# Two-block transformer on one core: residual pieces split before they are scaled, and weight refills issued earlier

## What is computed

```python
x = half_ffn(x, ffn_norm[l, 0], ...)
h = rmsnorm(x, mix_norm[l])
x = x + (mixer_gla_rglru(h, ...) if l == 0 else mixer_hgrn2(h, ...))
x = half_ffn(x, ffn_norm[l, 1], ...)
gate = sigmoid(rmsnorm(x, ple_norm[l]) @ ple_gate[l])
x = x + gate * (p[l] @ ple_proj[l])        # "PLE" below
```

## Time and profile before

| | us |
|---|---|
| runs | 2873.18, 2870.72, 2865.55 (median 2870.72) |
| the profiled execution | 2868.27 |
| its span | 2866.5 |
| TensorE matmul busy | 2717.7 (95%) |
| TensorE weight load busy | 2623.7 |
| DVE busy | 1380.7 (48%) |
| ACT busy | 1493.7 (52%) |
| GpSimd busy | 2206.3 (77%) |
| granted TensorE clock, mean | 0.975 |

### The profile page before, as it was taken

How to read it: one execution, slowest core, us unless ns; L and a number is a source line. 1 busy time by engine, 2 the same in 40 slices (tenths; PEclk the granted TensorE clock), 3 DMA queues, 4 the chain that set the end, 5 groups by cost and what they waited for, 6 DMA issues and landing times.

```text
span 2866.5 us, 60073 instructions
## 1 busy us (share of the span) xinstructions
PE 2717.7 (95%) x21805; PEld 2623.7 (92%) x21812; DVE 1380.7 (48%) x2501; ACT 1493.7 (52%) x2269; POOL 2206.3 (77%) x1681
## 2 busy tenths in 40 slices
PE   8999999999999999999989989999999899898997
PEld 8999988889999989898889989998999899788997
DVE  2125435646556554525556554346433733735335
ACT  4444455555555545455465554457545644555445
POOL 8876766757988967666858968978898699667994
PEclk9999999999999999999999999999999999999998
DMA  6544434434554544433434544544555355444552
GB/s 242 183 169 151 142 124 135 153 118 155 184 175 158 187 143 170 133 133 133 162 118 155 183 147 162 183 147 159 170 184 187 126 189 185 135 135 148 188 183 78
DMA packets 123000, 452.12 MB, mean 158 GB/s; under 512 B 13650, under 2 KB 13650, under 8 KB 122196
## 3 DMA queue, kind: packets, MB, share of 16 engines
q1 hardware_dynamic: 121104, 441.43, 45.8%
q10 hardware_dynamic: 1732, 8.39, 0.8%
HBM read 448.72 MB, written 1.05 MB: 157 GB/s over the span
## 4 chain that ended last, share of the span: by engine, by line
POOL 45%; PE 25%; issue 23%; DVE 5%; ACT 2%; POOLq 0%; DVEq 0%; ACTq 0%
POOL wl L372 23%; POOL wl L373 22%; PE R L407 6%; PE R L411 6%; PE R L410 6%; PE Y L407 1%; PE Y L411 1%; PE Y L410 1%; DVE M L2260 1%; DVE XLB L1904 0%; ACT wh L1140 0%; PE Y L647 0%; PE R L512 0%; DVE G L2259 0%; PE R L570 0%
## 5 line engine op out<-in xcount | busy, mean ns | idle before, releaser
L372 POOL TENSOR_TENSOR wl<-raw,wh 128x512 fp32r<-128x512 f32 x836 | 1112.3, 1331 | 639.1 <-ACT wh L1140 632.9
L407 PE MATMUL R<-XHB,wh 128*128 128x256 f32 (+1 forms) x4264 | 1218.8, 286 | 15.9 <-DVE XLB L2279 6.2
L411 PE MATMUL R<-XHB,wl 128*128 128x256 f32 (+1 forms) x4264 | 1209.5, 284 | 0.0
L410 PE MATMUL R<-XLB,wh 128*128 128x256 f32 (+1 forms) x4264 | 1205.6, 283 | 0.0
L373 POOL TENSOR_TENSOR wl<-raw,wh 128x512 fp32r<-128x512 f32 x836 | 1144.4, 1369 | 0.0
L1140 ACT ACTIVATE wh<-raw 128x1024 fp32r<-128x1024 f32 x836 | 877.3, 1058 | 298.8 <-PE R L407 218.8
L407 PEld LDWEIGHTS R<-XHB,wh 128*128 128x128 f32 x4264 | 810.9, 190 | 23.7 <-POOL wl L373 10.4
L410 PEld LDWEIGHTS R<-XLB,wh 128*128 128x128 f32 x4264 | 814.1, 191 | 1.8 <-issue 1.0
L411 PEld LDWEIGHTS R<-XHB,wl 128*128 128x128 f32 x4264 | 812.5, 191 | 0.0
L407 PE MATMUL Y<-BH,wh 128*128 128x256 f32 x1408 | 398.0, 283 | 1.3 <-DVE BL L1828 1.3
L411 PE MATMUL Y<-BH,wl 128*128 128x256 f32 x1408 | 396.4, 282 | 0.0
(11 more groups left out here) (402 smaller groups left out, 3187.9 us busy)
## 6 DMA issues: line engine op xcount, KB each, us to landing
raw<-in_stream SPq DMA_DIRECT2D x836, 512.0 KB, 3.3
G<-in_wcmp ACTq DMA_DIRECT2D x2, 2048.0 KB, 7.8
G<-in_mem ACTq DMA_DIRECT2D x2, 1024.0 KB, 7.2
TB<-in_table SPq DMA_DIRECT2D x1, 1312.0 KB, 12.4
X<-in_x SPq DMA_DIRECT2D x2, 512.0 KB, 5.1
out_dram<-X ACTq DMA_DIRECT2D x4, 256.0 KB, 2.2
WS<-in_mix_w ACTq DMA_DIRECT2D x2, 256.0 KB
G<-in_p ACTq DMA_DIRECT2D x2, 256.0 KB, 3.3
```

Of the source, the lines that this page charges most:

```text
L372: pool.tensor_tensor(wl[:, s, 0:512], raw[:, r, 0:512], wh[:, s, 0:512].bitcast(F32), ALU.subtract)
L407: i = pe.matmul(o, wh[w], hi, start=start, stop=False, skip_group_check=True)
L410: pe.matmul(o, wh[w], lo, start=False, stop=False, skip_group_check=True)
L411: i = pe.matmul(o, wl[w], hi, start=False, stop=stop, skip_group_check=True)
```

## The change

The pieces go unscaled to the first six blocks at ln1, gla and hgrn: three together, then the sum of squares, then three plain blocks, the last of which tells ACT of each piece that it has read (`piece_read`). DVE scales these six outputs by the root, and scales X into X or W8 by a copy of the root in PSUM (RS); ACT and DVE then overwrite XH and XL with the scaled pieces, from which the rest is made. In `gla` the order of chunks becomes lr, k, xr, xg. PLE's norm goes too: the projection comes first, the gates are made of unscaled pieces in BH and BL, and each gate output is scaled, passed through tanh and used in its PSUM bank; in layer 0 the next feed-forward's pieces are made per chunk (and its first product takes lead=6). `add_y` makes pieces as it adds; the last ln4 interleaves its pieces. `split_early` issues one refill ahead of a seam's pieces, on the end of the stage before.

```diff
-    return dict(xr=0, lr=4, k=5, xg=7, q=11, g=13)
+    return dict(lr=0, k=1, xr=3, xg=7, q=11, g=13)
...
+            def unscaled_six(hi, lo, width):
+
+                together(3, hi, lo, split_ready, width)
+                need(sq_added, 3)
+                for c in range(2):
+                    i = pe.matmul(SQ, ONES, W8[:, c, :], start=c == 0, stop=c == 1, skip_group_check=True)
+                i.then_inc(sum_ready, 1)
+                for _ in range(2):
+                    dense(hi, lo, width=width)
+                dense(hi, lo, width=width, passed=piece_read)
...
+                unscaled_six(XHB, XLB, T + 2)
                 together(3, XH, XL, split_ready)
-                for c in range(3, Z_N):
+                for c in range(3, 9):
+                    aside(c)
+                for c in range(9, Z_N):
                     dense(XH, XL)
                     aside(c)
...
+                unscaled_six(XH, XL, T)
                 together(3, XH, XL, split_ready)
-                for _ in range(3):
-                    dense(XH, XL)
                 evicted(c["lr"])
...
-                for _ in range(5):
+                for _ in range(2):
                     dense(XH, XL)
                 need(lconv_split)
...
-                together(3, XH, XL, split_ready)
-                for _ in range(5):
-                    dense(XH, XL)
+                unscaled_six(XH, XL, T)
+                together(2, XH, XL, split_ready)
                 tokens_major(XH, XL)
...
+            def split_early(s, value):
+
+                n = t.n["hi"]
+                act.wait_ge(raw_landed[n % RAW], t.up(("raw", n % RAW), 16))
+                act.wait_ge(s, value)
+                t.up("begun")
+                t.up("hi")
+                act.activation(wh[:, n % SPLIT, :], raw[:, n % RAW, :], ACT.Copy).then_inc(hi_done, 1)
...
+            def piece_again(c, src):
+
+                act.wait_ge(piece_read, t.up(piece_read))
+                give_dve(act.activation(XH[:, c, :], src, ACT.Copy))
...
+                late_root(0, keep=True)
+                skip(6)
+                split_next()
+                split_next()
+                biased(0)
+                biased(1)
+                step(biased(2))
+                split_next()
+                for c in range(4):
+                    i = shifted(c)
+                step(i)
+                aside(2)
+                for c in range(4, DC):
+                    i = shifted(c)
+                step(i)
+                split_next()
+                biased(3)
+                split_next()
+                biased(4)
+                for c in range(DC - 1):
+                    piece_again(c, X[:, c, :])
+                biased(5)
+                last_again(X[:, DC - 1, :])
...
+                late_root(1)
+                skip(6)
+                for _ in range(5):
                     split_next()
-                    skip(1)
-                column(c["lr"])
-                column(c["k"])
+                for j in range(DC - 1):
+                    need(x_scaled)
+                    piece_again(j, W8[:, j, :])
+                need(x_scaled)
+                last_again(W8[:, DC - 1, :])
                 split_next()
+                skip(1)
                 o = ready_of("gla", "gate")
...
+                late_root(1)
                 need(lb_shifted)
                 act.activation(LB[:, 0:2, :], LB[:, 0:2, :], ACT.Exp).then_inc(lb_exp, 1)
-                for c in range(8):
+                split_next()
+                split_next()
+                for c in range(3):
+                    from_dve()
+                    forget(c)
+                split_next()
+                split_next()
+                from_dve()
+                forget(3)
+                split_next()
+                from_dve()
+                forget(4)
+                for c in range(DC - 1):
+                    need(x_scaled)
+                    piece_again(c, W8[:, c, :])
...
-                norm(DC, xs, False, 1.0 / D, 1, None, XH, made=projected)
...
+                late_root(1)
                 for c in range(DC):
                     split_next()
+                    need(gate_scaled)
                     m, o = chunk()
-                    take(act.activation(W8[:, c, :], o[:, 0:T], ACT.Tanh, scale=0.5), m)
...
+                    give_dve(act.activation(o[:, 0:T], o[:, 0:T], ACT.Tanh, scale=0.5))
+                    if l + 1 < DEPTH:
...
+                        piece(c, following)
...
+            def scaled_again(gain):
+
+                step(dve.tensor_copy(RS, S3[:, 0:T]))
+                for c in range(DC):
+                    give(stt(W8[:, c, :], X[:, c, :], col(gain, c), RS, ALU.mult, ALU.mult), x_scaled)
+
+            def low_again(c, src):
+
+                from_act()
+                give_pe(tt_(XL[:, c, :], src, XH[:, c, :].bitcast(F32), ALU.subtract))
...
+                for c in range(3):
+                    scaled(c)
+                scaled_again("mix_g1")
+                scaled(3)
+                scaled(4)
+                for c in range(DC - 1):
+                    low_again(c, W8[:, c, :])
+                scaled(5)
+                low_again(DC - 1, W8[:, DC - 1, :])
                 need(lb_exp)
...
                 for c in range(DC):
-                    skip(1)
+                    m, o = chunk()
+                    give(tt_(o[:, 0:T], o[:, 0:T], S3[:, 0:T], ALU.mult), gate_scaled)
                     from_act()
-                    step(stt(M[:, c, :], W8[:, c, :], 1.0, M[:, c, :], ALU.add, ALU.mult))
-                    give_act(stt(X[:, c, :], M[:, c, :], 0.5, X[:, c, :], ALU.mult, ALU.add))
+                    step(stt(o[:, 0:T], o[:, 0:T], 1.0, M[:, c, :], ALU.add, ALU.mult))
+                    take(stt(X[:, c, :], o[:, 0:T], 0.5, X[:, c, :], ALU.mult, ALU.add), m)
```

More of the change, by code:

```diff
@@ L1208, in pieces @@
                     piece(c, gain)
+                    if c == 3 and early is not None:
+                        early()
             def last_splits(gain):
@@ L1253, in ffn @@
                     skip(1)
-                split_next()
+                if not early:
+                    split_next()
                 if kind != "first":
@@ L2001, in sharpen, with norm @@
                 take(stt(y, u, 1.5, y, ALU.add, ALU.mult), m)
-            def norm(n, src, mean, scale, eps, gain, bias, hi, lo, between=0, behind=0):
+            def norm(n, src, mean, scale, eps, gain, bias, hi, lo, between=0, behind=0, made=None):
                 if mean:
@@ L2038, in norm @@
                     low(n - 1)
+                elif made is not None:
+                    made(n - 1)
             def softmax(u, a):
@@ L2121, in rope, with scaled @@
                     return tt_(Z[:, c, :], Z[:, c, :], S1[:, :], ALU.add)
+                def scaled(c):
+                    m, o = chunk()
+                    step(tt_(Z[:, c, :], o[:, 0:T], S3[:, 0:T], ALU.mult))
+                    take(tt_(BQ[:, c:c + 1], o[:, T:T + 1], col(f"b_in{l}", c), ALU.add), m)
+                    dve.sem_inc(dve_act, 1)
+                    t.up(dve_act)
+                for c in range(3):
+                    scaled(c)
+                step(dve.tensor_copy(RS, S3[:, 0:T]))
+                for c in range(DC):
+                    give(stt(X[:, c, :], X[:, c, :], col(f"ln1_g{l}", c), RS, ALU.mult, ALU.mult), x_scaled)
+                for c in range(3, 5):
+                    scaled(c)
+                for c in range(DC - 1):
+                    low_again(c, X[:, c, :])
+                scaled(5)
+                low_again(DC - 1, X[:, DC - 1, :])
                 step(ts_(NB_IN[:, :], col(f"b_in{l}", Z_N, Z_GATES), 0.5, None, ALU.mult))
@@ L2342, in gla @@
                         take(i, m) if d == 3 else step(i)
+                late_root(RMS_EPS)
+                for z in (c["lr"], c["k"], c["k"] + 1):
+                    m, o = chunk()
+                    take(tt_(Z[:, z, :], o[:, 0:T], S3[:, 0:T], ALU.mult), m)
+                scaled_again("mix_g0")
+                conv(0)
+                conv(1)
+                for j in range(4):
+                    low_again(j, W8[:, j, :])
+                conv(2)
+                for j in range(4, DC):
+                    low_again(j, W8[:, j, :])
+                conv(3)
                 dve.sem_inc(lconv_done, 1)
```

183 lines of the change are left out of this document (118 added, 65 removed).

## The result

The changed kernel takes 2889.57 us (median; 2886.85 to 2890.68), the kernel before 2869.05 beside it: ratio 1.0070, 95% interval 1.0058 to 1.0082. It is slower by some 20 us where the forecast said 2868, no change; 2889.6 lies above the range, past its end of 2884. The profiled execution has a span of 2888.9 us against 2866.5 before.

The account below looks back on a forecast made before the run. PE was taken to set the pace, GpSimd's blocks ready just ahead, with PE's idle time at the seams. Terms -1.0 + 5.0 + 6.5 - 3.0 - 4.5 - 3.0 gave 0.0 against 2868.3 us; range 2846 to 2884.

Parts of the forecast that it names:

- forecast case: All seams: gains and losses of the terms cancel, 2868 us; chance 0.50, own range 2857 to 2880.
- rival 2: Mixer entries: second three-block product starves, block 9 after t = 19.5; 2880 us, 2888 with hgrn's chain slow; chance 0.17.
- ln1, -0.5 each: ln1, both layers: earlier start nearly lost waiting for block 9, at t = 16.6 from the sum of squares' start; -1.0 together.
- gla, +5.0: gla entry: five refills in a row, then the gate and block 11's late refill delay the token-major blocks; +5.0 us.
- hgrn, +6.5: hgrn entry: DVE's bounding of f starts later, behind scalings and low parts, delaying ACT's exps; +6.5 us.
- ln4, -3.0: ln4 of layer 1 into the feed-forward: early refill no longer falls between low parts; -3.0 us.
- PLE of layer 0, -4.5: PLE, layer 0: projection starts at once without the norm, gate chunks then 3.3 us each; -4.5 us.
- PLE of layer 1, -3.0: PLE, layer 1: the same without new pieces, last gate chunk earlier, tail of 16.4 us kept; -3.0 us.
- Early refills ahead of ln3 and ln4, 0: Three entries, ln3 and ln4 of layer 0: fourth block was ready in time, centring waits for sums; 0.
- Rival 1: Entries: refills keep up and the entries' gains stay; with half of the waits gone -22, 2846 us; chance 0.28.
- Rival 3: Unscaled entries: PE waits at the same instants, chunks waiting for the root hold the banks; within 3 us of 2868; chance 0.05.
- The estimate with an added drain at each table load (2874): Four roots that hold up refills: a 1.38 us drain per table switch, 5.5 us more, 2874 us; rejected from the trace.

Follow-up runs that it names:

- Late_early: Changed kernel with the early refill of gla and hgrn moved from behind the fourth unscaled piece to behind the last one; 2883.94 us, ratio 1.0055.
- f_delayed: Kernel before the change, with eight extra two-SBUF-operand subtractions on DVE in hgrn ahead of the bounding of f; 2872.07 us, ratio 1.0013.
- all_back: Changed kernel with the gla, hgrn and both ln1 entries as before; PLE, last ln4 and early refills stay changed; 2863.89 us, ratio 0.9975.
- gate_first: Changed kernel with gla's gate matmuls, gate copies, table load and two small logs ahead of the second scaled product; 2884.60 us, ratio 1.0041.
- mixers_back: Changed kernel with the gla and hgrn entries as before; ln1, PLE, last ln4 and early refills stay changed; 2867.06 us, ratio 0.9992.
- no_lows: Changed kernel with the second making of low parts (gla, hgrn, both ln1) touching one column in 256; 2881.65 us, ratio 1.0042.

## Why the prediction was wrong

**Sign of the result.** The forecast case had the mechanisms, and nearly every error was too small a loss. Its sum of 0.0 became +18.0 by stage. The time of 2889.6 is close to that given for rival 2 with hgrn's chain slow (2888), but by luck more than by its reasoning: block 9 came at t = 18.1 in ln1 and 17.1 in gla, before its point of decision of 19.5, and hgrn's bounding of f ran fast, not slow. The waits ahead of the second products, forecast at 4 to 6 us, were 5.2 and 6.7 in ln1, 3.0 in gla and under 0.5 in hgrn. The failing steps:

**ln1, -0.5 each, measured +3.6 and +2.3.** The failing number is "block 9 at 16.6". It came at 18.06: GpSimd ended block 8 at 15.25 instead of 14.1, since ACT reached that refill about 1.1 us later behind the shifts than forecast, and its last block took 2.85 us instead of 2.50. PE started its product at t = 18.4, the sum of squares stood 0.5 later than forecast, the product took 11.1 instead of 10.8. Then 1.3 to 1.5 that was not priced at all: ACT waits 6.1 us for the product's first chunk, has all three to serve at once, and PE waits 1.32 us for its squares (263.41). The plain second product gives that back (11.6 us from the product's end through the next blocks, instead of 13.0).

**gla, +5.0, measured +9.2.** Right: second product at 17.4 after the sum of squares (17.5 forecast), 10.2 us long (10.6). Wrong: "8.8 us as at the entry above, plus 1.5" for the pieces. The sum of squares came 13.7 us after the last down block, 2.9 later than forecast (10.8). In the earlier trace rows GpSimd was idle; here two refills from the feed-forward's end were still running, and DVE's first low parts took 1.15 and 0.91 us instead of 0.48. Late_early shows the early refill's share: 1.7, where 1.5 had been priced, so nearly all of the 2.9 is the rest: the last low part ended 12.4 us after the last down block (10.2 forecast), and an addition of squares of 0.69 us still stands between it and the sum. Behind the product "block 11 wanted 3.9 us after the product, there at 6.9" held: PE waited 2.8 there. What the sum lacked is 3.5 us from the gate to the token-major blocks, 17.0 instead of 13.5: about 1.8 is half clock behind that stall (36 matmuls from 1968.02 take 6.06 us, and 4.3 at 0.1185 each), and the wait of 2.06 us in the convolution's block, which the kernel before has too, has no term behind block 11.

**hgrn, +6.5, measured +9.8.** The mechanism, a later chain for f, held, and f_delayed shows it by itself. Its size held as well, values to outer product 37.4 us against 30.8, +6.6 where 6.4 had been worked out, but two errors cancel in it. The bounding began 3.6 us after the values' start (2508.64) instead of 0.4, since six small operations on the bounds that were not priced run ahead of it for 4.4 us; and it took 10.3 us to the end at 2518.93 instead of 13.5, because 13 of the 16 operations ran at 0.4 us, most of them while GpSimd was idle. The values started 22.4 us after the sum of squares (22 forecast). The miss is the sum of squares, 14.5 us after the last down block where the forecast's own numbers give 11.0 (2488.6 less 22, from 2455.6). Five other runs with the same entry have 13.7, so some 0.8 of it is this trace's. gla's account of the pieces fits here too, but no run separates it in hgrn.

**ln4, -3.0, measured -2.3**: right in nine of the thirteen traces with this code, and 0 to 1.3 in the other four. **PLE of layer 0, -4.5, measured -4.0**: right. **PLE of layer 1, -3.0, measured -0.6**: the last gate chunk ends 2.3 us earlier in the stage, and the tail, which the forecast kept, took 17.8 us instead of 16.2; with the same code it takes 14.9 in all_back and gate_first. **Early refills ahead of ln3 and ln4, 0**: ln3's stages moved by 0.4 and 0.5.

**The contention.** The forecast costed the scalings by the earlier trace rows, 0.51 us each even beside GpSimd, rightly. Those have one operand in PSUM. The low parts and additions of the pieces have two in SBUF; for them it took the quiet entry of the earlier trace rows plus 1.5, though the earlier trace rows had an addition at 1.65 us beside GpSimd. Beside it they took 0.8 to 1.7. The Trainium skill (SBUF — State Buffer, Who interferes with whom) says just that: a DVE instruction with two SBUF inputs contends with a GpSimd instruction that reads SBUF, one with at most one outside the faster modes doesn't. The rows agree on both halves: eight scalings 4.10 us, the addition of squares 1.67 against 0.69. One operand in SBUF is no safeguard by itself: the bounding's operations on one SBUF tensor take 0.41 us alone and 1.2 to 1.4 beside GpSimd.

**Rivals.** Rival 1 (2846) fell as its "against" said: no mixer entry kept its gain while refills waited behind the root. With refills moved ahead, ln1 (together with the plain product) and PLE do gain; gla and hgrn don't reach the kernel before in any run. Rival 3 didn't appear. The estimate with an added drain at each table load (2874) stays refuted in its step: the row 1964.35 begins at the end of the load at 1963.05, 1.28 us long.

## What to carry to other kernels

An entry that lets the matrix engine start early only moves the wait unless the refills and the elementwise chain of the next stage move with it: list, for each queue, what is first needed after the early start, and who is now behind it. Price an operation by a row with the same operand places and the same neighbour at work, not by its kind and size. Put a refill ahead of a wait in its queue where its slot is free before that wait ends, and look at what stands behind it: in ln1 that move alone gave nothing, in PLE of layer 1 it gave 3.5 us and in layer 0 it gave 0.7. Two moved refills with the plain product in ln1 and one moved refill in PLE were worth 6 and 7 us by the medians, and the reordering of gla and hgrn behind their products nothing.

## What was not expected of the hardware

The same stretch with the same wait does not take the same time. In layer 0's attention PE waits 2.8 to 2.9 us for DVE in each kernel. The windows hold the block of products ahead of that wait, the wait, and the matmuls behind it up to the same one, in the kernel before, the changed one and mixers_back; with each stands the row that ends the wait:

```profile
360.80:372.15 11.35, 8.51 (x38) 7.81 (x37) 3.18 (x7) 1.53 (x2) 2.52 (x2) 0.65 0.15 46
...
368.78 0.48 PE L637 MATMUL Y<-CAUS,IDB 128*128 128x384 bf16 x1 [2.84 <-DVE Z L2239]
```

```profile
365.65:376.66 11.01, 8.26 (x37) 7.57 (x37) 3.54 (x7) 1.53 (x2) 2.51 (x2) 0.65 0.16 49
...
373.87 0.32 PE L650 MATMUL Y<-CAUS,IDB 128*128 128x384 bf16 x1 [2.75 <-DVE Z L2392]
```

```profile
362.97:371.86 8.89, 5.99 (x37) 5.65 (x37) 3.23 (x7) 1.53 (x2) 2.53 (x2) 0.86 0.18 61
...
370.11 0.32 PE L650 MATMUL Y<-CAUS,IDB 128*128 128x384 bf16 x1 [2.90 <-DVE Z L2368]
```

The same 37 or 38 recorded matmuls are busy for 2.3 to 2.5 us less where the granted clock is 0.86 instead of 0.65, with nearly the same wait among them. There are many such stretches in an execution. The tail of the program behind the last gate chunk, the same code in twelve traces, takes 14.9 to 17.9 us, and the stage around it 49.0 to 53.6. So a stage read from one profile is uncertain by 1 to 3 us and at times by over 4, and only medians tell a term of that size. What makes the clock rise earlier in one execution than in another stays open. Whether it makes all of the 4 us in stages that no edit touches, and of the 4 us of no_lows in layer 1, is not shown.
